# A decoder step: expert rows multiplied during the expert choice as three fp32r products, with the remainders formed by GpSimd

## The reference

```python
def chunk_fn(xc):                       # xc = rms_norm(x), tokens x 1024
    q = (xc @ w_query).reshape(-1, 8, 256)                 # 8 heads
    s1 = einsum('chk,nk->chn', q[..., :128], keys1)        # 128 scores
    s2 = einsum('chk,nk->chn', q[..., 128:], keys2)        # 128 scores
    v1, i1 = top_k(s1, 16)
    v2, i2 = top_k(s2, 16)
    sc, ci = top_k(v1[..., :, None] + v2[..., None, :], 16) # of 256 sums
    eid = i1[ci // 16] * 128 + i2[ci % 16]                 # one of 16384 experts
    gate = softmax(sc)
    act = gelu(einsum('chkd,cd->chk', exp_u[eid], xc))
    return einsum('chk,chkd->cd', gate * act, exp_v[eid])
```

## Time and profile before

| | us |
|---|---|
| median of 3 runs | 1727.59 |
| lowest and highest | 1726.24, 1731.49 |
| profiled execution | 1730.63 |
| its span, first to last instruction | 1728.8 |
| TensorE busy | 1659.2 (96% of the span) |
| VectorE, ScalarE, GpSimd busy | 1338.5, 618.5, 453.7 |

### The profile page before, as it was taken

One profiled execution on the slowest core, in us unless ns is written; L12 is line 12 of the kernel. 1 busy time (PEld: TensorE's weight loads), 2 busy tenths in 40 slices (PEclk: granted clock), 3 DMA queues, 4 the chain that ended last, 5 costly groups with the idle time before them and its releaser, 6 DMA issues.

```text
span 1728.8 us, 24171 instructions
## 1 busy us (share of the span) xinstructions
PE 1659.2 (96%) x8587; PEld 1374.4 (80%) x8587; DVE 1338.5 (77%) x2697; ACT 618.5 (36%) x1034; POOL 453.7 (26%) x511
## 2 busy tenths in 40 slices
PE   7999988999999999978999999999999999999997
PEld 6777664476767679968999999999999999997774
DVE  5888553257898779957888888888888888887776
ACT  5332442121111168853333333333333333333333
POOL 1000000012322300013444444444444444443110
PEclk9999999999999999999999999999999999999998
DMA  8312813042221238898999999999999999999882
GB/s 280 119 68 99 306 38 116 0 151 65 83 70 42 73 89 253 239 295 303 346 336 347 347 339 339 362 332 350 338 354 346 337 350 349 335 353 319 277 301 76
DMA packets 164427, 411.53 MB, mean 238 GB/s; under 512 B 15503, under 2 KB 76461, under 8 KB 162893
## 3 DMA queue, kind: packets, MB, share of 16 engines
q1 hardware_dynamic: 118229, 242.20, 39.5%
q0 software_dynamic: 46080, 167.79, 27.5%
HBM read 375.34 MB, written 33.24 MB: 236 GB/s over the span
## 4 chain that ended last, share of the span: by engine, by line
PE 70%; DVE 6%; issue 3%; ACT 3%; DMA 1%; SPq 0%; DVEq 0%; ACTq 0%
PE bank L1423 25%; PE bank L1471 23%; PE bank L1410 7%; PE bank L1362 7%; PE bank L1340 3%; PE bank L1452 3%; DVE y0s L1977 2%; PE bank L1399 1%; ACT v_parts L1591 1%; DVE gel L1955 1%; DVE placed L1934 1%; DMA u<-in_uT 1%; ACT u_high L1591 1%; DMA gates_kept<-staged 1%; DVE hot_b L1927 0%
## 5 line engine op out<-in xcount | busy, mean ns | idle before, releaser
L1471 PE MATMUL bank<-v_parts,p_high 128*128 128x512 f32 x1404 | 437.2, 393 | 5.0 <-DVE v_parts L1911 4.5
L1471 PEld LDWEIGHTS bank<-v_parts,p_high 128*128 128x128 f32 x1404 | 261.5, 188 | 59.8 <-DVE v_parts L1911 12.0
L1679 POOL DMA_INDIRECT rows<-in_u_rows,row_u x160 | 195.4, 1221 | 403.1 <-DVE dots L1967 227.2
L1423 PE MATMUL bank<-h_high,u_high 128*128 128x384 f32 x832 | 283.2, 340 | 11.9 <-DVE u_low L1911 11.2
L1423 PE MATMUL bank<-h_low,u_high 128*128 128x384 f32 x832 | 283.3, 340 | 0.0
L1423 PE MATMUL bank<-h_high,u_low 128*128 128x384 f32 x832 | 279.0, 335 | 0.0
L1471 PE MATMUL bank<-v_parts,p_low 128*128 128x512 f32 x702 | 274.1, 390 | 0.0
L1679 POOL DMA_INDIRECT rows<-in_v,row_u x160 | 185.1, 1157 | 281.8 <-DVE y L1977 177.9
L1596 ACT CAST p_high<-gel 128x384 fp32r<-128x384 f32 x128 | 65.7, 513 | 496.0 <-DVE gel L1955 496.0
L1911 DVE TENSOR_TENSOR u_low<-u,u_high 128x1024 fp32r<-128x1024 f32 x115 | 140.8, 1224 | 40.5 <-ACT u_high L1560 36.9
L1911 DVE TENSOR_TENSOR v_parts<-vv,v_parts 128x1024 fp32r<-128x1024 f32 x117 | 143.4, 1226 | 36.5 <-ACT v_parts L1591 32.4
(11 more groups left out here) (235 smaller groups left out, 2428.3 us busy)
## 6 DMA issues: line engine op xcount, KB each, us to landing
vv<-in_v SPq DMA_DIRECT2D x117, 512.0 KB
u<-in_uT SPq DMA_DIRECT2D x104, 512.0 KB
gate<-gates_kept SPq DMA_DIRECT2D x30, 768.0 KB
gates_kept<-staged SPq DMA_DIRECT2D x11, 2048.0 KB, 9.9
early<-in_uT SPq DMA_DIRECT2D x24, 512.0 KB, 3.6
w_in_sb<-in_w_in SPq DMA_DIRECT2D x9, 1024.0 KB, 8.7
wq<-in_w_q SPq DMA_DIRECT2D x16, 512.0 KB, 3.7
ckT<-in_ckT SPq DMA_DIRECT2D x4, 1536.0 KB, 13.1
```

Of the source, the lines that this page charges most:

```text
L1423: ins = pe.matmul(a_ps[par][:, 0:DT], x[:, par, k], y, start=(k == 0 and n == 0), stop=(k == KT - 1 and n == 2))
L1471: ins = pe.matmul(y_ps[2 * (i - 1) + half][:], x[:, b, of], y[:, part], start=(t == 0 and n == 0), stop=(t == NK - 1 and n == 2))
L1679: nc.gpsimd.indirect_dma_start(rows[:, r % ROW_BUFS], None, table, bass.IndirectOffsetOnAxis(ap=row_u[:, s_:s_ + 1], axis=0)).then_inc(fet ...
```

## The change

- All 24 chunks of the choice are multiplied by `activate`, as three fp32r products. `activate_early` and the four `early` buffers are gone; the chunks go through the two buffers of `u`, and SP loads chunk q + 2 when chunk q is multiplied.
- ScalarE rounds them: in a head the first chunk behind the copies of the first half of the queries, the second behind those of the second half; in the tail chunk q + 2 behind the gelu of chunk q.
- GpSimd forms the remainders (`split_early`): two in a head, after the pick and ahead of the sums; in head 7 two more after the sums, and the others after the last pick.
- GpSimd multiplies the hits of a head at once, before the next head's splits and sums.
- h is rounded ahead of the first head, and its remainder is formed by GpSimd instead of VectorE. `h_low` has a place of its own; `h2T` moves to a region that ends with the choice; `tops`, `ef`, `gsum`, `shift` and `row_f` lie over buffers that are free by then.

```diff
+        h_low = base("h_low", [P, KT, DT], F32R)
...
             def load_u(q, par):
-                first = q < WHOLE + 2
-                sp.wait_ge(a_done, q - EARLY_BUFS + 1 if first else q - 1)
+                wait(sp, a_done, q - 1)
...
-            for q in range(EARLY_BUFS):
-                load_early(q)
+            for q in range(2):
+                load_u(q, q % 2)
...
                 for q in early_after(n):
+                    load_u(q + 2, q % 2)
...
             def activate(q, par, halves=(0, 1)):
                 if 0 in halves:
+                    if q == 0:
+                        pe.wait_ge(h_split, KT)
+                    if q < 2:
+                        pe.wait_ge(h0s_ready, 2)
+                    if q < WHOLE:
+                        pe.wait_ge(early_split, q + 1)
+                    else:
+                        pe.wait_ge(u_split, q - WHOLE + 1)
...
                 for q in early_after(n):
                     if q == WHOLE - 2:
                         turn_slots()
-                    activate_early(q)
+                    activate(q, q % 2)
...
# ScalarE, head(n), behind the copies of each half
+                    for q in early_after(n)[half:half + 1]:
+                        round_u(q, q % 2)
...
             act.wait_ge(h_taken, 2 * TILES)
+            for k in range(KT):
+                nc.scalar.copy(h_high[:, k], h2T[:, k, P:END]).then_inc(h_rounded, 1)
             for n in range(PH):
                 head(n)
-                for q in early_after(n)[:7]:
+                for z, q in enumerate(early_after(n)[:7]):
                     gelu(q)
+                    for q in early_after(n)[z + 2:z + 3]:
+                        round_u(q, q % 2)
...
# GpSimd
+            for k in range(KT):
+                pool.wait_ge(h_rounded, k + 1)
+                nc.gpsimd.tensor_tensor(h_low[:, k], h2T[:, k, P:END], h_high[:, k].bitcast(F32), ALU.subtract
+                                        ).then_inc(h_split, 1)
+            def split_early(q):
+                pool.wait_ge(u_rounded, q + 1)
+                nc.gpsimd.tensor_tensor(u_low[:, q % 2], u[:, q % 2], u_high[:, q % 2].bitcast(F32), ALU.subtract
+                                        ).then_inc(early_split, 1)
             for n in range(PH):
+                if n:
+                    pick(n - 1)
+                for q in early_after(n)[:2]:
+                    split_early(q)
                 for i in range(tiles_of(n)):
                     sums(n, i)
-                if n:
-                    pick(n - 1)
+            for q in early_after(PH - 1)[2:4]:
+                split_early(q)
             pick(PH - 1)
+            for q in early_after(PH - 1)[4:]:
+                split_early(q)
...
# VectorE, gates stage
-                if n == HOTS:
-                    dve.wait_ge(a_done, WHOLE)
-                    split_h()
```

More of the change, by code:

```diff
@@ L81 @@
 IN_HEADS = {0: 1, 1: 2, 2: 2, 3: 2, 4: 2, 5: 2, 6: 2, 7: 11}
-EARLY_BUFS = 4
 IN_GATES = EARLY - sum(IN_HEADS.values())
@@ L86 @@
 GEL_AT = TOP - RING * DT * 4
-assert 0 < IN_GATES < NB - 1 and WHOLE % EARLY_BUFS == 0 and NB % 2 == 0
+assert 0 < IN_GATES < NB - 1 and WHOLE % 2 == 0 and NB % 2 == 0
 LEAD = EARLY + 1
@@ L1069, in route @@
         h_high = base("h_high", [P, KT, DT], F32R)
-        at = base.at
-        h2T = base("h2T", [P, KT, T])
-        h_low = nc.alloc_sbuf_tensor_at("h_low", [P, KT, T], F32R, offset=at)
+        h_low = base("h_low", [P, KT, DT], F32R)
         gel = nc.alloc_sbuf_tensor_at("gel", [P, RING, DT], F32, offset=GEL_AT)
@@ L1080, in route @@
         g2_row = x_region("g2_row", [P, D])
+        late = Region(nc, base.at + TILES * D * 4, x_region.at)
         u_region = Region(nc, base.at, GEL_AT)
-        early = nc.alloc_sbuf_tensor_at("early", [P, EARLY_BUFS, KT, P], F32, offset=base.at)
         u, u_low = u_region.pair("u", "u_low", [P, 2, KT, P])
         u_high = u_region("u_high", [P, 2, KT, P], F32R)
-        assert u_region.at - base.at == EARLY_BUFS * KT * P * 4
         ident, catT = s.ident, s.catT
@@ L1099, in route @@
         keysT = sb("keysT", [P, 2, NK])
+        h2T = sb("h2T", [P, KT, T])
         qh = sb("qh", [P, 4, T])
@@ L1113, in route @@
         keyf = sb("keyf", [P, 2, 2, TILES, TOPK])
[L1114 to L1118, removed]
+        tops = late("tops", [P, TILES, PH, TOPK])
+        ef = late("ef", [P, 2, TILES, PH, TOPK])
+        gsum = late("gsum", [P, TILES, PH])
+        shift = late("shift", [P, TILES, PH, TOPK])
+        row_f = late("row_f", [P, FETCHED])
         spreads = sb("spreads", [P, PACK, NS])
@@ L1173, in route @@
         u_rounded, u_split = sem("u_rounded"), sem("u_split")
-        early_in = [sem(f"early_in{b}") for b in range(EARLY_BUFS)]
+        early_split = sem("early_split")
         gates_copied = [sem(f"gates_copied{b}") for b in range(2)]
@@ L1230, in load_query @@
                     sp.dma_start(wq[:, b], d.w_q[4 * it + b]).then_inc(wq_in[b], 16)
-            def load_early(q):
-                wait(sp, a_done, q - EARLY_BUFS + 1)
-                sp.dma_start(early[:, q % EARLY_BUFS], d.uT[q]).then_inc(early_in[q % EARLY_BUFS], 16)
             def load_u(q, par):
-                first = q < WHOLE + 2
-                sp.wait_ge(a_done, q - EARLY_BUFS + 1 if first else q - 1)
-                sp.dma_start(u[:, par], d.uT[bass.ds(q, 1)].rearrange("o p k e -> (o p) k e")).then_inc(u_in[par], 16)
+                wait(sp, a_done, q - 1)
+                sp.dma_start(u[:, par], d.uT[q]).then_inc(u_in[par], 16)
             load_query(0)
@@ L1401, in head @@
                     ins.then_inc(s_done, 1)
[L1403 to L1412, removed]
             def activate(q, par, halves=(0, 1)):
                 if 0 in halves:
-                    pe.wait_ge(u_split, q - WHOLE + 1)
+                    if q == 0:
[6 more added lines that the diff above has]
+                        pe.wait_ge(u_split, q - WHOLE + 1)
                     wait(pe, acted, q - 1)
-                    if q == WHOLE:
-                        pe.wait_ge(h_split, KT)
                 for k in range(KT // 2 * halves[0], KT // 2 * (halves[-1] + 1)):
-                    high, low = h_high[:, k], h_low[:, k, P:END]
+                    high, low = h_high[:, k], h_low[:, k]
                     for n, (x, y) in enumerate(((u_high, high), (u_high, low), (u_low, high))):
@@ L1539, in gelu, with round_u @@
                 nc.scalar.activation(gel[:, q], a_ps[q % 2][:, 0:DT], ACT.Gelu_apprx_tanh).then_inc(acted, 1)
+            def round_u(q, par):
+                act.wait_ge(u_in[par], 16 * (q // 2 + 1))
+                nc.scalar.copy(u_high[:, par], u[:, par]).then_inc(u_rounded, 1)
             act.wait_ge(h_taken, 2 * TILES)
+            for k in range(KT):
+                nc.scalar.copy(h_high[:, k], h2T[:, k, P:END]).then_inc(h_rounded, 1)
             for n in range(PH):
                 head(n)
-                for q in early_after(n)[:7]:
+                for z, q in enumerate(early_after(n)[:7]):
                     gelu(q)
-            for k in range(KT):
-                nc.scalar.copy(h_high[:, k], h2T[:, k, P:END]).then_inc(h_rounded, 1)
+                    for q in early_after(n)[z + 2:z + 3]:
+                        round_u(q, q % 2)
             act.wait_ge(shifted, 2)
@@ L1556, in whole @@
                                hot_b[:, n % 2].rearrange("p g k t -> p g t k")).then_inc(hot_made, 1)
[L1558 to L1562, removed]
+            for z, q in enumerate(early_after(PH - 1)[7:-1], 7):
                 gelu(q)
+                for q in early_after(PH - 1)[z + 2:z + 3]:
+                    round_u(q, q % 2)
             whole(0)
@@ L1911, in low @@
                 return nc.vector.tensor_tensor(part, whole, high.bitcast(F32), ALU.subtract)
-            def split_h():
-                for k in range(KT):
-                    low(h_low[:, k, P:END], h2T[:, k, P:END], h_high[:, k], h_rounded, k + 1).then_inc(h_split, 1)
             def split_u(q, par):
-                low(u_low[:, par], u[:, par], u_high[:, par], u_rounded, q - WHOLE + 1).then_inc(u_split, 1)
+                low(u_low[:, par], u[:, par], u_high[:, par], u_rounded, q + 1).then_inc(u_split, 1)
             for n in range(BATCHES):
-                if n == HOTS:
-                    dve.wait_ge(a_done, WHOLE)
-                    split_h()
                 if n % (GB // TB) == 2 and n // (GB // TB) in range(1, IN_GATES + 2):
```

## The result

| | before | after |
|---|---|---|
| median, us | 1727.3 (4 runs) | 1751.0 (4 runs: 1747.2 to 1753.3) |
| profiled execution | 1730.6 | 1749.9 |
| its span | 1728.8 | 1747.8 |

The ratio is 1.0132, 95% interval [1.0118, 1.0146]: slower by 23.7 us. The direction was forecast, and the rise of 11.9 was half of it. The median lies above the stated range, which ended at 1750.

What follows compares the result with a forecast made beforehand. TensorE alone was taken to bound the choice before the change. Heads -3.5, tail +13.3, gates' start -1.3 and clock +3.4 sum to +11.9 on the median 1727.6: 1739 us, range 1730 to 1750.

Steps and rivals of the forecast that it cites:

- rival (d): In heads and tail TensorE stays the bound and hides GpSimd's line: 1705 us; chance 0.06.
- the cycle of a pair: Late tail: load, rounding, split, product and hand-overs on two buffers make 11.4 us for two chunks, against 10.3 before.
- The gates' start: After the choice: h_low leaves VectorE's chain, 1.3 us back, bounds 0.6 and 3.84.
- the falls of the clock: TensorE at 1.2 GHz after new gaps: two falls counted, 1.7 us each, 3.4 together; bounds 0 and 10.
- the start of chunk 17: Tail: its split, behind head 7's pick, ready at x + 34.4 us; x is VectorE's first search of a head.
- VectorE's small steps: Between search and hits: run alone, not beside GpSimd's hits, they return 1.6 us a head to VectorE.
- Head 4: Late pick of ten hits: TensorE waits 5.3 us, VectorE 5.2; the head takes 32.3, 3.7 lost.
- the split's price: GpSimd's remainder of one chunk, in heads and tail: 2.1 us, between 1.9 and 2.5.
- heads: All heads of the choice together, gains of the others against head 4's loss: -3.5 us.
- tail without the clock: Choice after head 7: waits for splits and two buffers end it at x + 73.1 instead of 59.8, +13.3 us.
- the slope of the small instructions: Lower bound for a GpSimd split: 1.65 ns an element from sums of 56 and 8 elements, 1.9 us.
- four hits: Upper bound for a GpSimd split: four times a hit of 256 elements, 2.5 us; as a rival 1747, chance 0.16.

Runs made afterwards that it cites:

- the fillers: The changed kernel with unread products given to TensorE where it waited, ahead of chunks 7, 15, 17, 19, 21 and 23: 1744.5 us, ratio 1.0100.
- the plain tail: The changed kernel with the tail's eleven chunks as plain fp32 products again, without rounding or split: 1727.7 us, ratio 1.0007.
- four buffers: The changed kernel with four buffers instead of two for u and its rounded part in the choice: 1738.8 us, ratio 1.0063.
- the reordered kernel: The changed kernel with four buffers, roundings and splits as early as these allow, slots turned a chunk later, exps behind chunk 20's gelu: 1710.3 us, ratio 0.9901.
- `pick_behind`: The changed kernel, but GpSimd splits chunks 17 and 18 ahead of the pick of head 7 instead of behind it: 1744.5 us, ratio 1.0095.

## Why the prediction was right in its sign and short by half

**Right.** The rival (d), TensorE as the bound, fell where it was said to, at split 17. The waits were at the forecast places: chunk 15 8.84 (8), chunk 17 7.80 (7), the first two pairs 2.95 (2.8), VectorE's wait for the sums in head 4 6.14 (5.2). Of the loss, too, the tail was named as the place. With the clock up, the cycle of a pair took 11.56 (618.56 to 630.12), forecast 11.4. The gates' start gave back 1.9, forecast 1.3: the first gates product is 23.2 later, and the ninth batch (668.93 against 647.69) 21.2. The pace after it is nearly the same: 1078.9 to the end of the span, before 1081.1.

**What failed.** Two steps of the tail were sized too small: the falls of the clock (3.4, measured 6.6) and the start of chunk 17 behind the pick of head 7 (x + 34.4, measured x + 37.7), for which VectorE's small steps were taken to run alone. Head 4 and the split's price add the rest. By the steps, in us from x of head 0:

| step | forecast | profiled |
|---|---|---|
| heads | -3.5 | -0.4 |
| tail without the clock, and the clock | +13.3, +3.4 | +22.7 |
| gates' start | -1.3 | -1.9 |
| sum | +11.9 | +20.4 |

*The clock* and the start of chunk 17 are the two largest misses, of about the same size. Of the clock the prediction says: "I take two that count, 3.4; bounds 0 and 10." In the chain chunk 17 took 7.05, 21 6.02 and 23 6.00, each in place of the 4.45 of chunk 19. That is 5.7 in the tail, and just that much the fillers gave back there, with 0.9 in the heads: 6.6. Two of the three short pauses counted too (2.94 and 1.85 us), and not only the long ones, though the earlier trace rows had shown that one of 1.7 can be enough. It was a term sized wrong, within its bounds.

*The pick of head 7* started at x + 28.7 (595.41) and not x + 25.7. The prediction gave VectorE 1.6 us back for small steps that run alone. In the tail they don't: the splits of 15 and 16 now stand beside them, and one step took 2.12 us (586.84, above) until the second split ended. The 1.6 are returned in the heads only. The prediction also left out, in this place, the wait of VectorE for the sums that it had priced at 0.6 itself; it took 0.67 (572.12, above). Chunk 17 so started at x + 37.7 instead of x + 34.4. 3.3 and 5.7 make 9.0 of the 9.2 that the tail takes more than the 73.1 reckoned for it without the clock. These parts of the pick's delay are read from the trace; no run removes one of them alone.

*The split* at 2.365 instead of 2.1: normal heads took 27.5 (539.20 to 566.67) instead of 27.2, 0.3 each. Head 4 took 35.6 (476.92 to 512.49) instead of 32.3; its wait on VectorE's side was 0.9 longer, the rest came with the half clock from 484 to 491: with the fillers it took 33.1 (477.17 to 510.22). Head 5 then took 26.7, and 28.4 with the fillers, so that most of what the clock cost in head 4 came back at once. Of the two bounds, the slope of the small instructions (1.9) was too low, and four hits (2.5) too high. The estimate from "GPSIMD Engine Reference" of the Trainium skill (section 3.1), half of its time for 2048 elements, 2.25, came nearest, and is still 0.12 short.

The rest, from 20.4 by these steps to 23.7 in the medians, is that the profiled execution of before lay 3.3 above its median and that of after 1.1 below, less 1.1 from the starts and the loop.

The sign was no luck: the waits that the forecast was made of are there. That the loss was the tail's, and that it was made of order and buffers and not of the arithmetic, is shown by the plain tail, by four buffers, and by the reordered kernel. How the 6.6 of the clock divide among single pauses is read from one trace each, and not tested singly.

## What to carry to other kernels

When a cheaper product needs a chain of preparation (load, round, split), price the chain per buffer and compare it with the product: if the product before must free the buffer, they add. Put preparation a stage ahead, in the gaps of the engine that does it, and not in front of what the next engine waits for; here the same products and splits, in another order and with two more buffers, took 41 us less, of which the buffers alone gave 12. A pause on TensorE costs itself and, after most of the pauses here, what its clock loses, so a forecast of new pauses should charge both.

## What the runs showed of the hardware

- GpSimd's subtraction of 128 x 1024 fp32 elements takes 2.37 us, of 128 x 512 1.29; VectorE's takes 1.22 alone and 1.59 where it ran beside GpSimd's hits.
- VectorE's small integer step on 80 elements (0.19 us) took 2.12 us in the changed kernel and 2.81 in the reordered one (`ahead`; 2.72 of it in the chain above), until GpSimd's running split was done, while its searches beside splits kept their times (0.46 to 0.49 for two `MAX8`). The page "SBUF — State Buffer" of the Trainium skill (Who interferes with whom) tells of an exclusive lock between the two engines, which a `tensor_scalar` can need and which is held for a whole instruction. The durations agree.
- In the changed kernel TensorE's granted clock fell after pauses of 2.94 and 1.85 us, for 3.4 us each, and not after one of 2.96; with the pick behind (`pick_behind`) it did not fall after one of 2.82 (1.00 from 598 to 610). Around the pauses of 6.23, 8.84 and 7.80 us it was at the lower level for 6.8, 6.8 and 10.2 us. What decides for the short ones is open.
